# Attention in one core's kernel: a unit's values are multiplied one step behind its turns, through a ring of seven groups, and the maxima are taken in the order in which the score banks finish

## The reference, cut to what matters

```python
def _attend(q, k, v):
    s = jnp.einsum('bqkgd,bskd->bkgqs', q, k).astype(jnp.float32) * ATTN_SCALE
    p = jax.nn.softmax(s, axis=-1).astype(v.dtype)
    return jnp.einsum('bkgqs,bskd->bqkgd', p, v)
...
o_lat = lax.map(lambda qb: _attend(qb, k_all, v_all), q_blocks)   # 1024 queries over 1280 keys
y_b = o_lat... * jax.nn.silu(bz)
if with_ctx_out:                                                  # first layer only
    o_ctx = _attend(heads_q(bq_c), k_ctx, v_ctx)                  # 256 queries over 256 keys
...
mod_lat = silu_c @ w_ada[l] + b_ada[l]                            # modulation of each layer, from c
```

## Time and profile before

| | us |
|---|---|
| median of 3 runs | 4380.67 (4376.79 to 4384.58) |
| span of the profiled execution | 4384.1 |
| PE busy / DVE / ACT / POOL in it | 4058.8 / 1789.8 / 1356.9 / 639.9 |
| attention stage of layer 0 / layer 1 | about 325 / about 319 |

### The profile page before, as it was taken

The page is one execution under the profiler, slowest core; times in us unless marked ns, Lnnn a source line. Parts: engine busy times, 40 slices in busy tenths (PEclk is TensorE's granted clock), DMA queues, the critical chain, the costliest instruction groups (busy, mean ns, idle before and its releaser), DMA issues.

```text
span 4384.1 us, 47743 instructions
## 1 busy us (share of the span) xinstructions
PE 4058.8 (93%) x17556; PEld 2284.5 (52%) x17556; DVE 1789.8 (41%) x3853; ACT 1356.9 (31%) x3310; POOL 639.9 (15%) x846
## 2 busy tenths in 40 slices
PE   6999899989999899998999998999999999958995
PEld 3444566574444566664546666544666644433331
DVE  2443556273244455363244655211223301343445
ACT  3333455122233444222334444311223211211212
POOL 1012000020002000011022434101212200002331
PEclk8999999959999999968899999999999999979997
DMA  5001200022200231021201002000111100159885
GB/s 230 0 39 38 78 30 20 2 74 77 85 39 0 97 116 69 2 63 54 93 20 38 7 17 84 20 39 20 40 38 38 65 0 39 54 197 396 315 311 223
DMA packets 88196, 347.25 MB, mean 79 GB/s; under 512 B 20992, under 2 KB 52360, under 8 KB 69152
## 3 DMA queue, kind: packets, MB, share of 16 engines
q1 hardware_dynamic: 69536, 305.35, 18.6%
q0 software_dynamic: 18432, 38.85, 2.5%
HBM read 401.72 MB, written 37.83 MB: 100 GB/s over the span
## 4 chain that ended last, share of the span: by engine, by line
PE 81%; DVE 7%; ACT 5%; issue 3%; DMA 3%; POOL 1%; SPq 0%; POOLq 0%; DVEq 0%; ACTq 0%
PE psum L88 45%; PE psum L94 7%; PE psum L1870 5%; PE psum L894 4%; PE psum L873 4%; PE psum L3055 3%; PE psum L2097 2%; PE psum L3077 2%; DMA arena<-hn_scratch,arena 1%; ACT arena L955 1%; DMA arena<-w_ada 1%; PE psum L310 1%; PE psum L1270 1%; PE psum L2054 1%; PE psum L1801 1%
## 5 line engine op out<-in xcount | busy, mean ns | idle before, releaser
L88 PE MATMUL psum<-arena 128*128 128x512 f32 (+4 forms) x5280 | 2069.9, 550 | 30.4 <-DVE arena L2602 13.8
L88 PEld LDWEIGHTS psum<-arena 128*128 128x128 f32 x5280 | 990.2, 192 | 1028.3 <-issue 949.2
L94 PE MATMUL psum<-arena 128*128 128x128 f32 (+1 forms) x2866 | 455.8, 285 | 110.8 <-ACT arena L955 26.8
L94 PEld LDWEIGHTS psum<-arena 128*128 128x128 f32 (+1 forms) x2866 | 331.5, 144 | 303.9 <-issue 188.4
L1870 PE MATMUL psum<-arena 128*128 128x512 f32 (+1 forms) x640 | 290.3, 581 | 7.8 <-DVE arena L1898 4.4
L3055 PE MATMUL psum<-arena 128*64 x512 | 232.3, 608 | 22.5 <-issue 11.0
L3056 PE MATMUL psum<-arena 128*64 128x512 f32 x512 | 232.2, 608 | 0.0
L175 DVE SCALAR_TENSOR_TENSOR arena<-psum,arena 128x512 f32<-128x512 f32 (+1 forms) x100 | 60.6, 606 | 404.6 <-ACT arena L172 404.0
L170 ACT ACTIVATE arena<-psum 128x512 f32<-128x512 f32 (+1 forms) x100 | 53.1, 531 | 489.6 <-PE psum L88 489.6
L894 PE MATMUL psum<-arena 128*64 128x128 f32 x2624 | 203.0, 283 | 0.7 <-ACT arena L955 0.7
L955 ACT ACTIVATE arena<-psum 128x512 f32<-128x512 f32 x200 | 112.8, 597 | 252.3 <-PE psum L94 252.3
(11 more groups left out here) (389 smaller groups left out, 4719.4 us busy)
## 6 DMA issues: line engine op xcount, KB each, us to landing
arena<-w_gu SPq DMA_DIRECT2D x32, 2048.0 KB
arena<-w_ada SPq DMA_DIRECT2D x24, 2048.0 KB
arena<-w_dn SPq DMA_DIRECT2D x32, 1024.0 KB
arena<-w_in SPq DMA_DIRECT2D x12, 2048.0 KB
arena<-w_out SPq DMA_DIRECT2D x6, 2048.0 KB
arena<-gate_rows_scratch SPq DMA_DIRECT2D x36, 256.0 KB, 3.3
x_scratch<-arena SPq DMA_DIRECT2D x18, 512.0 KB, 2.9
arena<-x SPq DMA_DIRECT2D x16, 512.0 KB, 10.6
```

Source lines behind the costliest of these rows:

```text
L88: ins = e.matmul(out, l, r, start=(i == 0), stop=(i == n - 1))
L94: ins = e.transpose(o, i, idn)
```

## The change

- The values of a unit move one step later: step u of TensorE now issues the scores of u, the transposes of u - 1, the values of u - 2, and the turn of the output of u - 3. Within a step the order is: transposes of groups 0 and 1, values of groups 0 to 2, transposes of groups 2 and 3, values of groups 3 and 4, transposes of group 4, turn of the output.
- `PT` becomes a ring of seven groups (`PT_of`), counted over all units.
- VectorE copies groups 2, 3 and 4, ScalarE 0 and 1.
- VectorE takes the maxima of the second head's 1024 scores first, as soon as they are written (a new signal on the fourth score part), then the shared bank, then the first head's; ScalarE's exponentials go in the order head 1, head 0, and what waited for head 1's now waits for head 0's.
- The products of the output (L963 in the new file) and the statistics follow one unit later, with six slots for four.
- `Of`, the padded vector and the modulation row move into the key half of `KV`, which the stage no longer reads; the padded vector is laid out as 2 x 128 columns for 8 x 32.

```diff
+        def pad_of(pad, k):
+            return pad[:, k // 4, 32 * (k % 4):32 * (k % 4) + 32]
...
-        Pm, PT, sts = al(2, 2 * T), al(2 * T), al(4, 8)
-        Of, pad1 = al(2, 128), al(8, 32)
-        mrow1 = KV[:, 0:4, 0:128]
+        Pm, PT, sts = al(2, 2 * T), al(7, 512), al(6, 8)
+        mrow1, Of, pad1 = KV[:, 0:4, 0:128], KV[:, 4:6, 0:128], KV[:, 6:8, 0:128]
...
-            return (acop if g < 3 else vcop).of("PT", l, u, g)
+            return (acop if g < 2 else vcop).of("PT", l, u, g)
+
+        def PT_of(l, u, g):
+            return PT[:, (sum(att_tiles(l, i) // 2 for i in range(u)) + g) % 7, :]
...
+            def values(u, gs):
+                t, h = units[u]
+                ng = att_tiles(l, u) // 2
+                for g in gs:
+                    if g >= ng:
+                        continue
+                    e.wait_ge(*copied_P(l, u, g))
+                    if g == 0 and u:
+                        e.wait_ge(*acop.of("values", l, u - 1))
+...
...
-                        if (r, b_) in ((0, T), (0, n - 256), (1, 256)) or n < T:
+                        if (r, b_) in ((0, T), (0, n - 256), (1, 256), (1, T)) or n < T:
                             ins.then_inc(*prod.by("scores", l, u, r, b_))
-                    for g in range(min(2, ng)):
-                        turn_P(v, g)
-                    for g in range(ng):
-                        e.wait_ge(*copied_P(l, v, g))
-                        if g + 2 < ng:
-                            turn_P(v, g + 2)
-                        if g == max(0, ng - 2) and v:
-                            turn_values(v - 1)
-                        if g == 0 and v:
-                            e.wait_ge(*acop.of("values", l, v - 1))
...
+                v, w = u - 1, u - 2
+                ng = att_tiles(l, v) // 2 if 0 <= v < len(units) else 0
+                if ng:
+                    e.wait_ge(*aexp.of("att", l, v, 0))
+                for gs, ws in (((0, 1), (0, 1, 2)), ((2, 3), (3, 4))):
+                    for g in gs:
+                        if g < ng:
+                            turn_P(v, g)
+                    if 0 <= w < len(units):
+                        values(w, ws)
+                if ng > 4:
+                    turn_P(v, 4)
+                if w >= 1:
+                    turn_values(w - 1)
                 mul, tr = ada_steps(l, u)
...
                     if att_tiles(l, u) == NT:
+                        e.wait_ge(*prod.of("scores", l, u, 1, T))
+                        vo.seq(e, e.tensor_reduce(st[:, 3:4], S5[:, 1536:2560], AX, ALU.max))
+                        e.wait_ge(*prod.of("scores", l, u, 0, 1024))
+                        e.wait_ge(*prod.of("scores", l, u, 1, 256))
                         vo.seq(e, e.tensor_reduce(st[:, 0:2], P[2].rearrange("p (r n) -> p r n", r=2), AX, ALU.max))
...
-                    for g in range(3, att_tiles(l, u - 1) // 2):
+                    for g in range(2, att_tiles(l, v) // 2):
```

More of the change, by code:

```diff
@@ L309, in pe_ada @@
                 for j in range(4):
-                    ins = e.matmul(bank[32 * j:32 * j + 32, :], pad[:, 2 * j + s, :], w[:, 2 * j + s, :],
+                    ins = e.matmul(bank[32 * j:32 * j + 32, :], pad_of(pad, 2 * j + s), w[:, 2 * j + s, :],
                                    start=(s == 0), stop=(s == 1))
@@ L336, in program @@
         keep = al.at
-        mrow0, pad0 = al(4, 128), al(8, 32)
+        mrow0, pad0 = al(4, 128), al(2, 128)
         n_ss, n_sq = al(NT), al(1024)
@@ L857, in turn_P @@
                 bank_free[g % 2] = copied_P(l, u, g)
+            def values(u, gs):
[7 more added lines that the diff above has]
+                        e.wait_ge(*acop.of("values", l, u - 1))
+                    for j in range(2):
+                        for r in range(2):
+                            ins = e.matmul(P[7][64 * r:64 * r + 64, 0:128],
+                                           KV[:, 2 * g + j, 128 + 64 * (h // 4):192 + 64 * (h // 4)],
+                                           PT_of(l, u, g)[:, tile(2 * j + r)], start=(g == 0 and j == 0),
+                                           stop=(g == ng - 1 and j == 1))
+                    if g == ng - 1:
+                        ins.then_inc(*prod.by("values", l, u))
             def turn_values(u):
@@ L863, in turn_values @@
                 bank_free[1] = vmul.of("att", l, u)
-            for u in range(len(units) + 2):
+            for u in range(len(units) + 3):
                 if u < len(units):
@@ L924, in v_att @@
                     else:
-                        for r in range(2):
+                        e.wait_ge(*prod.of("scores", l, u, 0, 256))
+                        e.wait_ge(*prod.of("scores", l, u, 1, 256))
+                        for r in (1, 0):
                             vo.seq(e, e.tensor_reduce(st[:, 2 + r:3 + r], att_scores(l, u, r), AX, ALU.max))
@@ L950, in a_att @@
             units = att_units(l)
-            for u in range(len(units) + 1):
-                if u:
-                    for g in range(min(3, att_tiles(l, u - 1) // 2)):
-                        e.wait_ge(*turned.of("P", l, u - 1, g))
-                        e.activation(PT[:, half(g)], P[5 + g % 2], ACT.Copy).then_inc(*acop.by("PT", l, u - 1, g))
+            for u in range(len(units) + 2):
+                v, w = u - 1, u - 2
+                if 0 <= v < len(units):
+                    for g in range(min(2, att_tiles(l, v) // 2)):
+                        e.wait_ge(*turned.of("P", l, v, g))
+                        e.activation(PT_of(l, v, g), P[5 + g % 2], ACT.Copy).then_inc(*acop.by("PT", l, v, g))
                 if u < len(units):
-                    n, st = att_tiles(l, u) * 128, sts[:, u % 4, :]
+                    n, st = att_tiles(l, u) * 128, sts[:, u % 6, :]
                     if u > 1:
                         e.wait_ge(*turned.of("P", l, u - 2, att_tiles(l, u - 2) // 2 - 1))
-                    for r in range(2):
+                    for r in (1, 0):
                         e.wait_ge(*vsta.of("att", l, u, r))
```

61 lines of the change are left out of this document (24 added, 37 removed).

## The result

The changed kernel took 4354.42 us (median of 4 runs, 4353.34 to 4366.58) against 4382.32 for the kernel before: ratio 0.9942, 95% interval 0.9928 to 0.9957. Run once more on another occasion it took 4361.73 (9 runs, 4354.85 to 4368.68) against 4381.24 (12 runs): ratio 0.9958, interval 0.9948 to 0.9969. The forecast was 4356 in 4344 to 4374. The total is inside the range; what it is made of is right for single units and pairs and wrong for the clock, and part of the gain lies outside the change, as the rows show.

What follows compares the result with a forecast made beforehand. TensorE's own stream was taken to bound the kernel, the chain through scores, maxima and exponentials close behind. Terms -28.0 + 4.3 + 2.5 - 1.9 - 1.3 = -24.4 took 4380.7 to 4356 us, range 4344 to 4374.

Steps and rivals of the forecast that it cites:

- 16 pairs: Attention units carrying the modulation matmuls and the units after them with their turn: each pair 0.27 us slower, +4.3 in all.
- tails of both layers: End of attention: the last unit's values no longer run beside its transposes, +1.25 us in each layer, +2.5.
- heads (the first units of both layers): Start of attention: layer 1 saves 1.15 and 0.7 us, layer 0's short units 1, its first long one 0.3.
- The loss at each change of kind (3 x 0.17) and the covered wait: TensorE's unit: six runs for nine save 0.51 us, 24 values cover the 0.55 wait for ScalarE; period 7.57 for 8.57.
- the early maxima: VectorE's first reduction starts 2.13 us after the scores' start, bounds 1.86 to 2.56; at 2.56 a unit saves 0.71.
- The waits at the modulation: Behind group 4's transposes and the output's turn: products wait 0.8 us, unit 10.24; their turn's unit takes 10.01 against 9.55.
- So I count with 1.00: TensorE's clock stays full in the pairs, as their idle 0.8 and 1.5 in 10 us is a smaller share than before.
- The prediction's own sign: The forecast would be wrong if the clock in 500 to 750 us were under 1.00.
- rival (c): Waits in pairs drop TensorE to 1.2 GHz: four units hit (+27 us) cancel the gain, one per pair gives 4464; chance 0.06.
- Rival (a): Change-of-kind gaps return inside value runs or thin spares vanish: a unit saves 0.5 to 0.7, total 4371; chance 0.15.
- (b): The waits at the modulation matmuls and their turn cost nothing, so every unit saves 1.00: total 4320; chance 0.05.
- (d): The scores' chain, not TensorE, sets the period and the maxima's new order gives nothing: total 4380; chance 0.04.

Runs made afterwards that it cites:

- the first trace: Trace from the changed kernel's first measurement, 4354.42 us (median of 4 runs), set against the kernel before.
- second trace: Changed kernel measured once more, with no edit, on another occasion: 4361.73 us (9 runs), ratio 0.9958 to the kernel before.

## Why the prediction was right, and where it was not

By its own terms, against the first trace (attention 17.0 us shorter):

| term | forecast | measured |
|---|---|---|
| 28 long units without modulation | 28 x 1.00 = -28.0 | 28 x 0.98 = -27.5 |
| 16 pairs | 16 x 0.27 = +4.3 | 16 x 0.10 = +1.6 |
| half clock behind pairs | 0 | +8.8 (second trace +17.8) |
| tails of both layers | +2.5 | +5.6 |
| heads (the first units of both layers) | -3.2 | -5.3 (second trace -1.2) |
| outside attention | 0 | -14.2 (second trace -23.0) |

In attention the forecast is -24.4; measured are -17.0 and, in the second trace, -3.9.

- **The loss at each change of kind (3 x 0.17) and the covered wait: right.** A unit is 7.59 for the forecast 7.57; two changes put back cost 0.30. The bounds for the early maxima (1.86 to 2.56, taken 2.13) held: 2.03. The spare behind the exponentials was larger than worked out (0.52 for 7.57 - 7.33 = 0.24), since the first reduction starts 0.10 earlier and the second exponential starts 0.25 and not 0.40 behind its scalar step. The 0.40 was read from the first exponential; in the earlier trace rows the second one starts when the first has ended (614.43 + 1.32), so they don't show how soon it could.
- **The waits at the modulation: right in place and in kind, 0.1 and 0.1 too long.** That they come from their place behind the last transposes is shown by moving them (18.42 for 20.08) and by ScalarE's copy (9.28 for 9.90).
- **"So I count with 1.00": the step that failed.** The argument was that the earlier trace rows show TensorE idle for a larger share in a stretch at full clock. That stretch holds one long wait of the kernel before:

```profile
482.79 2.42 PE L873 MATMUL psum<-arena 64*128 64x256 f32 x12 [1.18 <-ACT arena L962]
```

One wait without a fall behind it says little: the four traces with a long wait before each turn (1.26, or 1.13 with the maxima in the old order) have a fall behind 18 of their 64 pairs, not counting the first pair of each. Without that wait there is none behind any of 32 pairs (turn moved), and with it at 0.64 none behind 15. The prediction's own sign came, too: from 500 to 750 us the granted clock is 0.99 in the first trace and 0.96 in the second, and under 1.00 was to mean wrong. The rival (c) had this mechanism and the breaking point (four units at 6.75 us). What a fall costs is 1.6 to 3.3 us, since the clock is back within the unit, not the whole unit's 6.75. It took a third to two thirds of the units' gain. The Trainium skill, "TensorE: Matmul & The Clock Gate", Part 4 (PE-mode transpose), says that transpose-mode matmuls don't count as busy for the clock in the same way. That may be part of it; by themselves the transposes don't bring the clock down here, as the kernel with both modulation steps moved has nearly the same runs of them and no fall behind a pair. No run takes them away and leaves the waits.
- **The tails: term mis-sized, 2.8 for 1.25.** I counted the values that stand alone and the output's turn, not the two waits for VectorE that the next unit's scores cover everywhere else.
- **The outside: not forecast.** Without it the first trace would have been at about 4367 and the second at 4380 by their spans, the latter beyond the range. That 4356 was met so closely is luck: an open gain of 14.2 stands in for 8.8 lost by the clock and 3.1 in the tails.

Rival (a) is excluded by the units' 7.59, (b) by the waits, (d) by both. Two versions beat both kernels clear of their spread: with both modulation steps behind the scores 4325.06, with the turn alone 4327.01. ScalarE's copy of group 4 gave 4344.78 in its one run.

## What to carry to other kernels

Where an instruction holds a PSUM bank, look at what stands behind it in the rare steps too: a reordering that is free in the common unit took away the values that stood in front of the modulation steps and covered their waits, and each pair lost the gain of both its units. A wait costs more than its length if the clock falls behind it, so a new wait of about 1 us on a TensorE that is otherwise hardly idle should be priced with some of the units behind it partly at half clock (1.6 to 3.3 us each time here), or moved. And compare the parts of the program that weren't touched before a total is taken as proof of a sum.

## What the runs showed of the hardware

- Going from transposes to products or back costs TensorE 0.15 to 0.17 us at full clock, whether the wait there is met or not; waits for other engines inside a run of one kind (16 or 24 value instructions) cost nothing once met. Whether it is the kind or the other shape that costs it, no run separates.
- The clock fell to half 0.6 to 2.4 us after the start of the modulation's turn that had waited 1.13 to 1.26 us, in stretches of 50 us in which TensorE was busy for 48, but behind 18 of 64 such waits only. It fell behind the one wait of 0.99 there too. It never did in the pairs with 0.68 alone or with 0.58 and 0.64.
- How often it falls differs between executions of the same kernel (8.8 and 17.8 us in two traces).
